# Raw token rows transposed as they land, their normalization factor applied behind the projections, first scores one slab later, in a hybrid encoder trunk

## What is computed

```python
xn = h * rsqrt(mean(h * h) + EPS) * norm_g        # RMSNorm, one factor for each token
z  = xn @ w_in                                     # 2048 x 16384
hy_in, hy_gate, fn_in, fn_gate, qkv, na_gate, merge = split(z)
u, x1, x2 = split(short_conv(hy_in))               # width-3 convolution along the tokens
y_a = hyena(u, x1, x2) * silu(hy_gate)             # two gated long convolutions
y_b = fourier(fn_in) * silu(fn_gate)               # 2-D DFT, real part
y_c = attention(q, k, v) * silu(na_gate)           # neighbourhood attention, 16 heads
m   = sum over branches of sigmoid(merge_i) * (y_i @ w_i)
out = rmsnorm(h + m @ w_out)[16:]
```

## Time and profile before

| | |
|---|---|
| median of 3 runs | 1156.02 us |
| the profiled execution's own time | 1155.4 us |
| its span in the trace | 1153.6 us |
| instructions | 17302 |
| mean granted clock of TensorE | 0.997 |
| HBM read, written | 195.19 MB, 5.24 MB |

### The profile page before, as it was taken

The page is one execution under the profiler, slowest core; times in us unless marked ns, Lnnn a source line. Parts: engine busy times, 40 slices in busy tenths (PEclk is TensorE's granted clock), DMA queues, the critical chain, the costliest instruction groups (busy, mean ns, idle before and its releaser), DMA issues.

```text
span 1153.6 us, 17302 instructions
## 1 busy us (share of the span) xinstructions
PE 1120.5 (97%) x7222; PEld 1013.8 (88%) x7222; DVE 765.9 (66%) x1141; ACT 560.9 (49%) x771; POOL 59.5 (5%) x98
## 2 busy tenths in 40 slices
PE   5999999999999999999999999999999999999997
PEld 3898999999999999999999988888888888888886
DVE  6767788668788587886887865554554455455554
ACT  6545645555555455554465464444444443444443
POOL 4011000300000300002000000000000000000000
PEclk9999999999999999999999999999999999999999
DMA  8635333553435533435544375555555555556652
GB/s 307 232 122 178 132 125 131 179 207 113 147 119 170 190 128 134 147 129 174 183 146 142 124 264 190 198 189 189 182 188 187 199 193 182 182 189 243 260 184 110
DMA packets 30494, 201.56 MB, mean 175 GB/s; under 512 B 3872, under 2 KB 4192, under 8 KB 7744
## 3 DMA queue, kind: packets, MB, share of 16 engines
q1 hardware_dynamic: 25024, 180.16, 44.7%
q0 software_dynamic: 5248, 19.77, 5.0%
q10 hardware_dynamic: 144, 0.52, 0.1%
HBM read 195.19 MB, written 5.24 MB: 174 GB/s over the span
## 4 chain that ended last, share of the span: by engine, by line
PE 84%; DVE 9%; issue 3%; ACT 3%; DMA 0%; ACTq 0%; DVEq 0%
PE ps L563 26%; PE ps L565 26%; PE ps L564 26%; DVE w_lo L1298 2%; ACT w_hi L978 1%; PE ps L568 1%; DVE k_lo L1298 1%; PE ps L587 1%; DVE sd L1390 1%; DVE hm L1385 1%; PE ps L717 1%; DVE q_two L1496 1%; DVE u L1484 0%; PE ps L677 0%; DVE prod L1533 0%
## 5 line engine op out<-in xcount | busy, mean ns | idle before, releaser
L1298 DVE TENSOR_TENSOR w_lo<-raw,w_hi 128x1024 fp32r<-128x1024 f32 x336 | 407.6, 1224 | 281.4 <-ACT w_hi L978 280.1
L978 ACT ACTIVATE w_hi<-raw 128x1024 fp32r<-128x1024 f32 x336 | 351.1, 1057 | 373.7 <-PE ps L565 372.9
L563 PE MATMUL ps<-xn_hi,w_hi 128*128 128x272 f32 (+2 forms) x1280 | 367.7, 287 | 0.0
L565 PE MATMUL ps<-xn_hi,w_lo 128*128 128x272 f32 (+2 forms) x1280 | 365.6, 286 | 0.0
L564 PE MATMUL ps<-xn_lo,w_hi 128*128 128x272 f32 (+2 forms) x1280 | 365.6, 286 | 0.0
L563 PEld LDWEIGHTS ps<-xn_hi,w_hi 128*128 128x128 f32 x1280 | 242.5, 189 | 2.1
L564 PEld LDWEIGHTS ps<-xn_lo,w_hi 128*128 128x128 f32 x1280 | 242.1, 189 | 0.8
L565 PEld LDWEIGHTS ps<-xn_hi,w_lo 128*128 128x128 f32 x1280 | 242.2, 189 | 0.0
L563 PE MATMUL ps<-w_hi,xn_hi 128*128 128x512 f32 x384 | 152.3, 397 | 0.0
L565 PE MATMUL ps<-w_hi,xn_lo 128*128 128x512 f32 x384 | 150.9, 393 | 0.0
L564 PE MATMUL ps<-w_lo,xn_hi 128*128 128x512 f32 x384 | 150.6, 392 | 0.0
(11 more groups left out here) (245 smaller groups left out, 1355.7 us busy)
## 6 DMA issues: line engine op xcount, KB each, us to landing
raw<-w_stream SPq DMA_DIRECT2D x168, 1024.0 KB, 4.9
branch_y<-ystage POOLq DMA_DIRECT2D x12, 256.0 KB, 3.2
y_raw<-branch_y POOLq DMA_DIRECT2D x3, 1024.0 KB, 7.1
xin<-x SPq DMA_DIRECT2D x2, 1024.0 KB, 7.1
w4s<-w POOLq DMA_DIRECT2D x16, 128.0 KB, 4.5
absd<-decay POOLq DMA_DIRECT2D x8, 256.0 KB, 6.5
h<-x POOLq DMA_DIRECT2D x2, 1024.0 KB, 9.4
rows_t<-rpb POOLq DMA_DIRECT2D x8, 219.0 KB, 6.2
```

Of the source, the lines that this page charges most:

```text
L563: mm(out_ap, a_hi, b_hi, start=first, stop=False)
L565: return mm(out_ap, a_lo, b_hi, start=False, stop=last)
L978: A(w_hi[:, w % 2, part, :], raw[:, w % 4, 1024 * part:1024 * part + 1024], ACT.Copy).then_inc(hi_done, 1)
L1298: return V.tensor_tensor(dst, src, hi.bitcast(F32), ALU.subtract)
```

## The change

- SyncE no longer waits for x before it issues slabs 0 to 3, and the identity goes ahead of x.
- The token rows are no longer scaled. TensorE transposes the raw rows: for k below 4 the first half of x and the meta tokens as soon as they have landed, then the second half; k from 4 to 7 before the last small matmul. The sums of squares write their unused output to SBUF; the sum of the second half comes later, under the first slab.
- The factors of all tokens are made later (`deviations`, ahead of the last four transposed tiles), spread out (`dev_rows`), transposed (`turn_deviation`) and kept as `dev_t`, the same row of 272 factors in every partition.
- Each evacuation begins with a VectorE pass that multiplies the PSUM pair by `dev_t` into one buffer, `stage` (for v it writes v itself); ScalarE and VectorE then read `stage` where they read PSUM before. The merge gates get the factor as the scale of the sigmoid, in two instructions for one.
- The first scores follow slab 7, and head 0's softmax moves from iteration 6 to 7.
- The sums and differences of filter part 2 and its low part move one place ahead; the turning of u's transform in iteration 11 comes ahead of the evacuation of x2.
- GpSimd builds the bias tile of chunk 0 after the first filter matmuls and ahead of the first store.

```diff
 SyncE
+            sp.dma_start(ident[:, :], ident_in).then_inc(ident_landed, 16)
             sp.dma_start(xin[:, 0, :], x[0:128, :]).then_inc(x_landed[0], 16)
             sp.dma_start(xin[:, 1, :], x[128:256, :]).then_inc(x_landed[1], 16)
-            sp.dma_start(ident[:, :], ident_in).then_inc(ident_landed, 16)
-
-            sp.wait_ge(x_landed[1], 16)
...
 GpSimd
             pool.wait_ge(xt_mm, KT)
+            pool.wait_ge(x_sq, 3)
...
             load_filter(1)
+            pool.wait_ge(kx_mm, 1)
+            make_bias(0)
             store_y(0, 1, yb_done)
-            make_bias(0)
...
 TensorE
+            def turn_part(k, t):
+                p, n = TOK[t]
+                part = nc.tensor.transpose(ps[:, 4 + k % 4, p:p + n], xin[0:n, t, 128 * k:128 * k + 128], ident[0:n, 0:n])
+                if t == 1:
+                    part.then_inc(xt_mm, 1)
+
+            def turn_deviation():
+
+                pe.wait_ge(dev_rowed, 3)
+                for t, (p, n) in enumerate(TOK):
+                    last = nc.tensor.transpose(ps[:, 5, p:p + n], dev_rows[0:n, t, :], ident[0:n, 0:n])
+                last.then_inc(dev_mm, 1)
...
-            pe.wait_ge(meta_scaled, 1)
-            pe.wait_ge(x_scaled, 1)
-            pe.wait_ge(x1_scaled, 1)
-            turn_x(range(4))
+            pe.wait_ge(x_landed[2], 16)
+            pe.wait_ge(x_landed[0], 16)
+            for k in range(4):
+                turn_part(k, 0)
+                turn_part(k, 2)
+            pe.wait_ge(x_landed[1], 16)
+            for k in range(4):
+                turn_part(k, 1)
+            turn_x(range(4, 8))
             mlp_matmul(2)
-            turn_x(range(4, 8))
             first_slab()
...
             make_h4(0, 1)
+            turn_deviation()
             proj_slab(1, 0, 1, 0)
...
-                    if t == 6:
+                    if t == 7:
                         pe.wait_ge(proj_read, blocks_read(c, "k"))
...
 ScalarE
             square(2)
             sine(0)
-            deviation(2, 1)
             square(0)
-            deviation(0, 2)
-            square(1)
-            deviation(1, 3)
-            sine(1)
             act.wait_ge(small_landed, 32)
             turned_high(range(2))
+            sine(1)
+            turned_high(range(2, 4))
             split(0, 0)
-            turned_high(range(2, 5))
+            turned_high(range(4, 6))
             split(0, 1)
-            turned_high(range(5, 8))
+            turned_high(range(6, 8))
+            square(1)
...
             A(hid_s[0:HID, :], hid[:, :], ACT.Copy).then_inc(hid_hi, 1)
+            deviations()
             turned_high(range(12, KT))
...
             def evac(c, name, b):
-                bank = bank_of(c, b)
-                act.wait_ge(half_used, halves_of(c, b))
+                if name != "fin":
+                    act.wait_ge(staged, blocks_staged(c, name))
...
-                A(mgate[:, m % 2, :, :], ps[:, pair:pair + 2, :], ACT.Sigmoid).then_inc(gate_done, 1)
+                for tt in range(2):
+                    ins = A(mgate[:, m % 2, tt, :], ps[:, pair + tt, :], ACT.Sigmoid, scale=stat[:, 12 + tt:13 + tt])
+                ins.then_inc(gate_done, 1)
...
-                    if t == 3:
-                        turned(c * 3 + 1, t_hi, uT_hi[:, 0:2, :], uT_hi[:, 2, :], 4, t_mm)
+                    if t in (7, 9, 11, 13):
+                        soft(c, (t - 7) // 2)
+                    if t in (3, 11):
+                        turned(c * 3 + (1 if t == 3 else 3), t_hi, uT_hi[:, 0:2, :], uT_hi[:, 2, :], 4, t_mm)
                     if t % 2 and BLOCKS[t // 2][0] != "v" and (c < LAST or t not in (15, 19)):
                         evac(c, BLOCKS[t // 2][0], t // 2)
...
 VectorE
+            def deviations():
+                dve.wait_ge(x_std, 2)
+                V.reciprocal(stat[0:NM, 14:15], stat[0:NM, 10:11])
+                link(V.reciprocal(stat[:, 12:14], stat[:, 8:10]))
+                for t, (p, n) in enumerate(TOK):
+                    V.tensor_copy(dev_rows[0:n, t, :], stat[0:n, 12 + t:13 + t].broadcast_to([n, 128])).then_inc(dev_rowed, 1)
...
                     if at_ == (3, 0):
                         sd_low(a, 1)
+                        sum_and_difference(a, 2)
                     if at_ == (3, 1):
-                        sum_and_difference(a, 2)
-                    if at_ == (3, 2):
                         sd_low(a, 2)
...
             def evac(c, name, b):
-                bank = bank_of(c, b)
-                src = ps[:, bank:bank + 2, 0:L]
-                src16 = ps[:, bank:bank + 2, 0:NG]
+                bank, width = bank_of(c, b), BLOCKS[b][2]
+                dve.wait_ge(half_used, halves_of(c, b))
+                by = dev_t[:, :, L - width:L].broadcast_to([128, 2, width])
                 if name == "v":
-                    dve.wait_ge(half_used, halves_of(c, b))
-                    V.tensor_copy(v[:, :, :], src).then_inc(proj_read, 1)
+                    V.tensor_tensor(v[:, :, :], ps[:, bank:bank + 2, 0:L], by, ALU.mult).then_inc(proj_read, 1)
                     return
+                V.tensor_tensor(stage[:, :, 0:width], ps[:, bank:bank + 2, 0:width], by, ALU.mult).then_inc(staged, 1)
+                dve.wait_ge(staged, blocks_staged(c, name))
                 if name == "fin":
-                    fold_fin(c, src, b)
+                    fold_fin(stage)
                 else:
                     dve.wait_ge(a_ev, copies_made(c, name))
...
-                        return V.scalar_tensor_tensor(dst[:, i, to], ps[:, bank + i, frm],
+                        return V.scalar_tensor_tensor(dst[:, i, to], stage[:, i, frm],
...
                 if p == 1:
+                    dve.wait_ge(dev_mm, 1)
+                    link(V.tensor_copy(dev_t[:, 0, :], ps[:, 5, 0:L]))
                     evac(-1, "fin", 7)
```

More of the change, by code:

```diff
@@ L98, in blocks_read, with blocks_staged @@
     before = 2 + c * NBLK + BLOCK_AT[name] + 1
+    return before - 1 if c == LAST and name == "ngate" else before
+def blocks_staged(c, name):
+    before = 2 + c * (NBLK - 1) + ("u", "q", "k", "x1", "x2", "hgate", "fin", "ngate", "fgate").index(name) + 1 if c >= 0 \
+        else ("fin", "fgate").index(name) + 1
     return before - 1 if c == LAST and name == "ngate" else before
@@ L268, in build @@
     v = place("v", [128, 2, L])
+    at[0] = fold_at
+    stage = place("stage", [128, 2, L])
     at[0] = fold_end
@@ L289, in build @@
     u = place("u", [128, 2, L])
+    prod_at = at[0]
     prod = place("prod", [128, 3, 2, CC])
+    prod_end = at[0]
+    at[0] = prod_at
+    dev_rows = place("dev_rows", [128, 3, 128])
+    at[0] = prod_end
+    dev_t = place("dev_t", [128, 1, L])
     at[0] = xin_at
@@ L353, in build @@
         x_std = sem("x_std")
-        x_rstd = sem("x_rstd")
-        x_scaled = sem("x_scaled")
-        x1_scaled = sem("x1_scaled")
+        dev_rowed = sem("dev_rowed")
+        dev_mm = sem("dev_mm")
+        staged = sem("staged")
         xt_mm = sem("xt_mm")
@@ L583, in turn_x @@
                         pe.wait_ge(xt_lo, k - 3)
-                    if k == 8:
-                        pe.wait_ge(x1_scaled, 2)
-                    for t, (p, n) in enumerate(TOK):
-                        last = nc.tensor.transpose(ps[:, 4 + k % 4, p:p + n], xin[0:n, t, 128 * k:128 * k + 128],
-                                                   ident[0:n, 0:n])
-                    last.then_inc(xt_mm, 1)
+                    for t in (0, 2, 1):
+                        turn_part(k, t)
+            def turn_part(k, t):
[8 more added lines that the diff above has]
+                last.then_inc(dev_mm, 1)
             def make_h4(g, tt):
@@ L1119, in evac @@
                     for i in range(2):
-                        ins = A(dst[:, i, p0:L], ps[:, bank + i, 0:L - p0], ACT.Identity,
+                        ins = A(dst[:, i, p0:L], stage[:, i, 0:L - p0], ACT.Identity,
                                 bias=params[:, bass.ds(c * 2 + (CB + t0 + i), 1)],
@@ L1127, in evac @@
                         ins = A(q_two[r, hh, :].rearrange("p (r n) -> p r n", r=4),
-                                ps[r, bank + hh // 2, 0:NG].rearrange("p (r n) -> p r n", r=4)[:, :, ::-1], ACT.Copy, scale=0.125)
+                                stage[r, hh // 2, 0:NG].rearrange("p (r n) -> p r n", r=4)[:, :, ::-1], ACT.Copy, scale=0.125)
                 elif name == "k":
@@ L1132, in evac @@
                         for rows in (0, 64):
-                            ins = A(k_hi[rows:rows + 64, odd:HC:2, 0:L], ps[64 * odd:64 * odd + 64, bank:bank + 2, 0:L], ACT.Copy)
+                            ins = A(k_hi[rows:rows + 64, odd:HC:2, 0:L], stage[64 * odd:64 * odd + 64, :, :], ACT.Copy)
                     ins.then_inc(khi_done, 1)
@@ L1146, in evac @@
                         act.wait_ge(s_mm, c * HC + HC)
-                    ins = A(gate[:, :, :], src16, ACT.Tanh, scale=0.5)
+                    ins = A(gate[:, :, :], stage[:, :, 0:NG], ACT.Tanh, scale=0.5)
```

(18 more changed lines are left out.)

48 lines of the change are left out of this document (14 added, 34 removed).

## The result

The changed kernel takes 1199.8 us (median of 5 runs, 1197.9 to 1201.6) against 1156.1; the ratio is 1.0369 [1.0352, 1.0385]. It is slower, as forecast, and by 16 us more than forecast: the range ended at 1193. All runs compared are fast ones; the kernel before falls into two groups among them (1155.6 to 1157.2 us and 1158.9 to 1159.8), so the base of a ratio moves by up to 0.3% with their mix.

The account below looks back on a forecast made before the run. TensorE was taken as the bound, with one stretch per chunk set by VectorE with ScalarE. 1155.4 - 5.1 (start) + 19.4 (slab 8) + 8.1 (second halves) + 5.7 (clock) = 1183.5, forecast 1184 us with the median's 0.6; range 1163 to 1193.

Parts of the forecast that it names:

- the clock term: TensorE after the 5 us stands at slab 8: half-rate matmuls cost 1.4 for each of four, +5.7 us (0 to 7.8).
- the sum: Whole kernel: 1155.4 - 5.1 (start) + 19.4 (slab 8) + 8.1 (second halves) + 5.7 (granted clock) = 1183.5 us.
- the second half of a chunk: After x2, hgate and fin, the h4 matmul waits for o: +2.7 us in chunks 0 to 2, +8.1 in all.
- The list of stands for chunk 1: TensorE in chunk 1: idles some 1.3 us before the scores and 5.0 before slab 8, in place of 1.5 and 0.3.
- the delay above it: Slab 8: low part 6.7 us later, less a margin of 1.0, so slab 8 starts 5.7 us later.
- The parts: Passes ahead of slab 8's low part: u +1.8, q +1.3 and k +3.6 us per chunk.
- Rival 3: Slab 8 of each chunk: passes fit into VectorE's idle third, so the kernel gets faster, 1142 us; chance 0.10.
- Rival 2: VectorE's taps and low parts: reading `stage` is faster than reading PSUM, taking half the time, 1159 us; chance 0.06.
- The start: Kernel start: first slab at 17.5 for 24.25, -6.7 us; with time given back, -5.1 in all (-6.7 to -2).
- Rival 4: Kernel start: slabs compete with the token rows, which land up to twice as late; 5.1 is lost, 1189 us; chance 0.04.
- the rival in which the clock holds: TensorE's long stands: the granted clock stays at its higher level through them, 1178.4 us; chance 0.22.

Follow-up runs that it names:

- b_pass: Kernel before, plus a multiplication by a row of ones into `stage` at each evacuation and the two moves this forces: 1215.5 us, ratio 1.0492.
- a_nopass: Changed kernel with every evacuation but v's reading PSUM directly, no pass into `stage`; token factor left out there: 1144.2 us, ratio 0.9876.
- b_moves: Kernel before with only the moves outside the start (later scores and softmax, earlier sums and turning, bias tile moved), no passes: 1147.8 us, ratio 0.9915.
- a_warm: Changed kernel with unread matmuls in TensorE's stands at slab 8 and ahead of the fin channels: 1187.6 us, ratio 1.0250.
- a_nopass_k: Changed kernel with k's evacuation alone reading PSUM directly, without its token factor; all other passes stay: 1181.7 us, ratio 1.0207.
- a_spwait: Changed kernel with SyncE's wait for the token rows put back ahead of the first slabs: 1198.9 us, ratio 1.0351.
- b_warm: Kernel before with the moves outside the start, parts 0 and 2 transposed first, and unread matmuls in TensorE's early pauses: 1149.1 us, ratio 0.9928.
- a_warm2: Changed kernel with unread matmuls in TensorE's stands within the chunks and at the start too: 1186.8 us, ratio 1.0250.

## Why the prediction was right, and where it failed

**The stands: right.** Without the clock term the sum was +22.4, 0.5 of it added transposes: 21.9 us more of TensorE standing still. Measured: 21.8. In chunk 1 I forecast about 1.3 ahead of the scores and 5.0 ahead of slab 8; measured 1.35 and 4.93. For the second half of a chunk I forecast 2.7; measured 2.1 for u at the fin channels, a few matmuls ahead of h4, and 0.2 to 0.4 more in short waits for o. The list of stands for chunk 1 did not fit the delay above it: 1.3 and 5.0 in place of 1.5 and 0.3 are 4.5 more, and slab 8 was to be 5.7 later. The missing 1.2 are the stands of 0.63 and 0.54 for `hm` and `folded`, which I had not seen; with them chunk 1 has 5.6 more. They are absent in chunk 0, where the stands grew from 3.8 (1.53 for `folded`, 0.74 for `sd_rest`, 1.49 for k) to 6.3, by 2.5 for the 2.3 forecast. The parts came out as priced too: k 3.3 for 3.6, u and q together 3.0 for 3.1.

**Rival 3, faster through VectorE's idle third: wrong.** The 36 passes take 25.2 us of VectorE (26 forecast); it is busier by only 21.5, since the scaling of the rows and the operation of 3.85 us are gone. Its share stays 66%, and the passes cost the time anyway. Rival 2 fell too: k's low part took 2.93 from PSUM and takes 2.92 from `stage`; q's taps took 1.73 and take 1.72. The advice that I set against the trace (the Trainium skill, VectorE: DVE Perf Modes, "Rules for kernel authors": copy PSUM to SBUF first where many operations follow) brings nothing here; `b_pass`, which is such a copy (a multiplication by ones) with the two moves that it forces, costs 4.9%.

**The start: right in its steps, a little dear.** I forecast the first slab at 17.5 and -5.1 in all. It began at 18.01, h4 at 32.22 (37.14 before), the first filter matmul at 56.37 (60.23 before):

```profile
9.17 3.59 PE L603 MATMUL ps<-ident,xin 128*128 128x128 f32 x12
...
18.01 0.59 PE L577 MATMUL ps<-xn_hi,w_hi 128*128 128x272 f32 x1
...
23.62 2.35 PE L603 MATMUL ps<-ident,xin 128*128 128x128 f32 x12
25.73 0.37 PE L577 MATMUL ps<-xn_hi,w_hi 128*128 128x272 f32 x1
...
32.22 0.51 PE L629 MATMUL ps<-w_hi,hid_s 128*128 128x512 f32 x1 [1.11 <-DVE xn_lo L1369]
...
56.37 0.36 PE L577 MATMUL ps<-sd_hi,filt_hi 128*128 128x256 f32 x1 [1.72 <-issue]
```

So 3.9 of the 5.1 arrive at 56. What I had not seen is between the second and the third row: the first slab, which begins 6.2 us earlier, stays at half pace for 5.7 us instead of 2.9, and gives 1.4 us back. The twelve transposes of the third row already run at full pace (2.35 us, against 3.38 for twelve at 16.52). Another 1.1 is lost between h4 and the filter, of which the longer stand, 1.72 for 1.24, is 0.5. Rival 4 (slabs compete with the rows) did not happen. GpSimd's bias additions, now at 57.66, still meet VectorE, at the splitting of two slabs from 56.67:

```profile
57.66 4.71 POOL L515 TENSOR_TENSOR bias_t<-rows_t,mask 128x384 f32<-128x384 f32 x4 [13.70 <-PE ps L582]
```

```profile
56.67 3.10 DVE L1321 TENSOR_TENSOR w_lo<-raw,w_hi 128x1024 fp32r<-128x1024 f32 x2 [0.40 <-ACT w_hi L1006]
```

3.10 in place of 2.36, so 0.7, and the evacuation of the gate at 61.54 takes 1.38 for 0.69 elsewhere: 1.4 in all where 3.4 was lost, and TensorE waits for neither. `a_nopass` and `b_moves`, which have the move, lack the 1.5 us wait for `folded` in chunk 0.

**The clock: the step that failed.** Direction and mechanism were right (the rival in which the clock holds fell), the size was not: 5.7 forecast, 13.8 measured by `a_warm` and 15.6 by the trace. All of the miss lies in TensorE's busy time, 22.1 us more for the 6.2 (5.7 and 0.5) of the sum. "I take 1.4 for each of four stands: +5.7 (0 to 7.8)" had two errors:
- *The number of stands.* I counted the four at slab 8. The three at the fin channels, 2.1 us each, were in my own sum (as 2.7), and I left them out because they were shorter than 5. The clock fell at all seven, and behind the 1.72 at the first filter matmul, which I had left out too.
- *The price of one.* I took it from the start of the kernel, where a matmul stretch of 2.9 or 3.9 us ran at half pace. The stretches behind slab 8 were 5.0, 3.8, 5.2 and 3.8 us long, half of which is lost each time, 8.9 in all; the three others, 3.3, 6.8 and 3.2 us long, lost 6.7. `a_warm` gives back 13.8 of these 15.6, with an interval of about 2.5 either way.

With the first slab's 1.4 and about 1.7 behind the stand at 56 (window 56 to 63, mean clock 0.76), that is 18.7 of the 21.6 us that TensorE is busier. The remaining 2.9 I cannot assign.

The range failed for the same reason. Its upper end took the clock term at 7.8, four stands at half of the longer of the two rows, 3.9; it should have asked what each stand of the sum, however short, could cost if the clock fell behind it.

## What to carry to other kernels

Price an added pass where two in-order engines hand work to each other: the pass serializes what ran side by side, so k's evacuation grew by the pass and by nearly all of ScalarE's part of it (3.3 us for an instruction of 0.72), whatever the shares of busy time say. Count TensorE's stands, not only their sum: here 33 us of stands came with 22 us more of busy TensorE (`a_nopass` against after), most of it matmuls at half pace, so a term for the clock belongs behind each of them, down to those of 2 us, as a cost that may come and not one that must. And take a change apart before dropping it: the moves in this one, freed of the passes, made the kernel 0.9% faster than before.

## What the runs showed that I had not expected

- The clock fell behind stands of 2.1 us (in the changed kernel and in `a_nopass_k`) and of 1.72; in these runs it did not behind those of 1.35 to 1.49 ahead of the scores. The length of the stand does not settle it alone. `a_nopass_k` has four stands of 2.99, and the clock fell behind three of them and not behind the fourth, at 617.7; in `a_warm2` it fell behind one of 0.76, at 687. It can also differ from one execution to the next: at the stand of 1.11 ahead of h4 it fell in the kernel before and in the changed one, and not in `a_nopass`, `a_warm` and `a_spwait`. The Trainium skill (TensorE: Matmul & The Clock Gate, "HAM oscillation — how this bites in real kernels") tells of it as the fate of long waits for data at every tile, and I had read it as a rule for the stands of 5 us alone; the rows here show that far shorter ones pay as well. `a_nopass_k` shows a fall most plainly, around its first stand of 2.99 (windows, columns as above):

```profile
118.00:124.00 6.00, 3.08 (x25) 2.86 (x23) 4.20 (x8) 3.65 (x5) 0.00 (x0) 1.00 0.49 178
124.00:126.00 2.00, 1.93 (x11) 1.96 (x12) 1.97 (x8) 1.51 (x2) 0.00 (x0) 0.68 0.34 139
126.00:130.00 4.00, 4.00 (x26) 4.00 (x26) 3.60 (x6) 2.18 (x5) 0.00 (x0) 0.73 0.00 0
```

  The clock is 1.00 during the stand and falls after it, when TensorE is busy again. In the stands of 4.9 of the changed kernel it falls before the stand ends, as the window up to 296.40 above shows.
- In the first slab the granted clock reads 1.00 while the matmuls run at half pace: one began every 0.23 us (18.40, 18.63, 18.86), and every 0.125 later. The trace of the changed kernel has no entry of the clock ahead of 23.7 us, and the views count its absence as 1.00. At the start of a kernel the spacing of the matmuls has to be read, not the clock's row.
- Unread matmuls in TensorE's stands hold the clock and give back more than they cost: in `a_warm` TensorE has 240 more of them, and the kernel is 12 to 14 us faster than without them. In `b_warm` 24 of them brought nothing: the fall at 37 is gone, and another, of the same 3.4 us, follows the first filter matmul, whose stand has grown from 1.24 to 2.65.
